# Four passes become one sequence of 64 steps, with the layer's output projection behind them

## What is computed

```
h  = rms_norm(x, g);  xx = token_shift(h) - h
xr, xw, xk, xv, xa, xg = (h + xx * mu[j] for j in range(6))
r, k, v, g = xr @ w_in[0], xk @ w_in[1], xv @ w_in[2], xg @ w_in[3]     # 1024 -> 2048
decay: from w0 + tanh(xw @ w1) @ w2          # low rank 64
a    = sigmoid(a0 + (xa @ a1) @ a2)          # low rank 64
S_t  = S_{t-1} diag(w_t) - (S_{t-1} kk_t)(a_t kk_t)^T + v_t k_t^T;  y_t = S_t r_t   # 32 heads of 64
y    = (head_group_norm(y) + bonus) * silu(g)
x    = x + y @ w_out                          # 2048 -> 1024, the output projection
x    = x + short_conv_mix(rms_norm(x))        # second layer, then further layers
```

## Time and profile before

| | |
|---|---|
| median of three timed runs | 4807.78 us (4807.76 to 4808.15) |
| the profiled execution | 4804.66 us, span of its trace 4802.9 us |
| PE busy | 4343.6 us, 90% of the span |
| DVE busy | 2354.9 us, 49% |
| ACT busy | 1297.8 us, 27% |
| POOL busy | 272.9 us, 6% |
| `rwkv_block` | 0 to about 2593 us of the span |
| DMA queues | 289.75 MB, of it 7.87 MB of instructions (queues q8 and q14) |

### The profile page before, as it was taken

The page is one execution under the profiler, slowest core; times in us unless marked ns, Lnnn a source line. Parts: engine busy times, 40 slices in busy tenths (PEclk is TensorE's granted clock), DMA queues, the critical chain, the costliest instruction groups (busy, mean ns, idle before and its releaser), DMA issues. The chain is left out here.

```text
span 4802.9 us, 134675 instructions
## 1 busy us (share of the span) xinstructions
PE 4343.6 (90%) x58154; PEld 3248.0 (68%) x58154; DVE 2354.9 (49%) x5293; ACT 1297.8 (27%) x3040; POOL 272.9 (6%) x304
## 2 busy tenths in 40 slices
PE   6999989998989998999987999999978988876669
PEld 5888768886478886788853887888755643444444
DVE  4555455553055554555522444344344551588952
ACT  2232223222022332233211333223212321433221
POOL 1000000000000000000000000000000000111100
PEclk9999999998999998999998999999989999567689
DMA  2222222221322221222223332333311110000010
GB/s 70 75 67 66 66 56 67 66 73 58 97 56 75 67 66 48 75 67 66 75 64 97 103 100 83 96 97 96 87 44 29 27 42 9 0 0 1 0 44 35
DMA packets 519184, 289.75 MB, mean 60 GB/s; under 512 B 29008, under 2 KB 508480, under 8 KB 518656
## 3 DMA queue, kind: packets, MB, share of 16 engines
q1 hardware_dynamic: 516352, 277.68, 20.6%
q10 hardware_dynamic: 2304, 4.20, 0.2%
HBM read 271.74 MB, written 8.39 MB: 58 GB/s over the span
## 5 line engine op out<-in xcount | busy, mean ns | idle before, releaser
L348 PE MATMUL a_bank<-a_lerps,a_wt 128*128 128x256 f32 x3072 | 790.6, 393 | 6.2 <-DVE a_lerps L834 2.7
L348 PEld LDWEIGHTS a_bank<-a_lerps,a_wt 128*128 128x128 f32 x3072 | 554.4, 190 | 96.3 <-DVE a_lerps L834 14.0
L1082 PE MATMUL b_bank<-b_hR,b_wR 128*128 128x512 f32 x1024 | 399.9, 391 | 24.7 <-DVE b_wL L1087 24.7
L1082 PE MATMUL b_bank<-b_hR,b_wL 128*128 128x512 f32 x1024 | 399.8, 390 | 0.0
L1082 PE MATMUL b_bank<-b_hL,b_wR 128*128 128x512 f32 x1024 | 399.7, 390 | 0.0
L949 DVE TENSOR_TENSOR a_iv_X<-a_bank,a_iv_X 128x256 f32<-128x256 f32 x256 | 108.7, 425 | 482.8 <-PE a_bank L448 475.6
L348 PE MATMUL a_bank<-a_hT,a_wt 128*128 128x256 f32 x1024 | 264.0, 391 | 0.0
L1087 DVE TENSOR_TENSOR b_wL<-b_w,b_wR 128x1024 fp32r<-128x1024 f32 (+1 forms) x144 | 192.5, 1341 | 117.0 <-ACT b_wR L1177 104.2
L1082 PEld LDWEIGHTS b_bank<-b_hR,b_wR 128*128 128x128 f32 x1024 | 193.2, 189 | 66.3 <-issue 25.9
L708 ACT ACTIVATE a_iv<-a_bank 128x512 f32<-128x512 f32 x192 | 114.6, 597 | 444.0 <-PE a_bank L454 268.1
L628 PE MATMUL a_bank<-a_yT,a_wt 128*128 128x512 f32 x512 | 227.9, 604 | 4.2 <-DVE a_t_sg L1026 4.2
(11 more groups left out here) (449 smaller groups left out, 8110.8 us busy)
## 6 DMA issues: line engine op xcount, KB each, us to landing
a_wt<-in_a_w_in SPq DMA_DIRECT2D x256, 512.0 KB, 4.4
b_w<-in_b_w_in SPq DMA_DIRECT2D x128, 512.0 KB, 4.0
a_wt<-in_a_w_out SPq DMA_DIRECT2D x16, 1024.0 KB, 6.8
b_w<-in_b_w_out SPq DMA_DIRECT2D x16, 1024.0 KB, 5.8
s_wp<-in_w_in SPq DMA_DIRECT2D x12, 512.0 KB, 3.8
a_xtok<-in_x SPq DMA_DIRECT2D x4, 1024.0 KB, 6.8
a_lerps<-in_x SPq DMA_DIRECT2D x2, 2048.0 KB, 9.1
x1t<-a_ends ACTq DMA_DIRECT2D x16, 256.0 KB, 6.1
```

Source lines behind the costliest of these rows:

```text
L348: r = mm(o, wt[:, j, c, :], src[:, c, :], start=(c == 0), stop=(c == ND - 1))
L1082: m = nc.tensor.matmul(o, a, b, start=(first and i == 0), stop=(last and i == 2))
```

## The change

The 64 steps are written out in one sequence (`steps`), with no hardware loops, no register values and no `at_tiles` waits; each step but the last makes the projections of the one after it, across the pass boundaries too. `before` and `first` are left only once, ahead of step 0. The preparation of the next pass is spread over the steps of the current one (`prepared`; `at` is the step's number in its pass): x is loaded at step 3, its squares summed on ACT at 8 (`squares`), the factor made on DVE and POOL and x scaled on DVE at 9, x transposed on PE in four parts at 9 to 12 (`turn_x`), shifted on POOL and mixed on DVE at 10 to 13 (`shift`, `lerped`, now four mixed inputs in a second buffer), and multiplied by the low-rank factors at 14 (`low_in`). The two low-rank products of a step, which had 128 rows each with half of them zeros, have 64 rows each, one on the upper and one on the lower half, and write to banks 0 and 6.

`y` goes to DRAM step by step (`store`, 128 KB). A new `mix_block` behind all steps loads it in 32 chunks of 128x512 through four slots, splits it into R and L parts (one ACT and one DVE instruction each), and makes the output projection for all 1024 tokens: 8 blocks of rows, each in 2 stages of 48 fp32r products, and 8 products for the residual. Beside them it makes the squares and sums for `conv_block`'s norm, whose `x1t` load and norm "1" are gone.

```diff
+        def steps(first, step):
+
+            first(0)
+            for n in range(STEPS):
+                step(n, n % 2, n % NF, n + 1 if n + 1 < STEPS else None, n - 1 if n else None)
+
+        def prepared(n):
+
+            ps, p = n // NF + 1, n % NF
+            return (ps, p) if ps < NPS else (None, None)
...
+                def store(n):
+                    sp.wait_ge(s["tail"], n + 3)
+                    sp.dma_start(yd[n % NF * P:(n % NF + 1) * P, n // NF * PASS:(n // NF + 1) * PASS], ybuf[n % 2][:, :]).then_inc(s[f"yst{n % 2}"], 16)
...
+                    if m >= 3:
+                        store(m - 3)
+                    if m % NF == 3 and m // NF + 1 < NPS:
+                        load_x(m // NF + 1)
...
+                def turn_x(ps, i, bk):
+
+                    pe.wait_ge(s["xsc"], ps + 1)
+                    for c in (2 * i, 2 * i + 1):
                         for b in range(PASS // P):
...
+                            o = c % 2 * PASS + b * P
+                            r = nc.tensor.transpose(bank[bk][:, o:o + P], xtok[:, b, c * P:(c + 1) * P], ident[:, :])
+                    r.then_inc(s["xT"], 1)
...
+                def low_in(ps, lo, hi, bk=0):
+
+                    for c in range(lo, hi):
+                        pe.wait_ge(s["hTe"], ps * ND + c + 1)
+                        mm(bank[bk][:, 0:PASS], lwa1[:, c, :], hT[:, c, 1:PASS + 1], start=(c == 0), stop=False)
+                        r = mm(bank[bk][:, 0:PASS], lwa1m[:, c, :], hT[:, c, 0:PASS], start=False, stop=(c == ND - 1))
+                    if hi == ND:
+                        r.then_inc(s["lwa"], 1)
...
                 def low_rank(m):
                     pe.wait_ge(s["wk"], (m + 1) * 48)
                     pe.wait_ge(s["bdR"], m + 1)
-                    mm(bank[0][:, 0:PASS], lwa2[:, 0, :], hwa[:, :], start=True, stop=True)
-                    mm(bank[0][:, PASS:], lwa2[:, 1, :], hwa[:, :], start=True, stop=True).then_inc(s["pwa"], 1)
+                    pe.wait_ge(s["hwa"], m // NF + 1)
+                    pe.wait_ge(s["hTe"], 2 * turned[0])
+                    if m >= 2:
+                        pe.wait_ge(s["H"], m - 1)
+                    mm(bank[0][:, 0:PASS], lwa2[w_rows, :], hwa[w_rows, :], start=True, stop=True)
+                    mm(bank[6][:, 0:PASS], lwa2[a_rows, :], hwa[a_rows, :], start=True, stop=True).then_inc(s["pwa"], 1)
 
...
+                    if prep and 9 <= at <= 12:
+                        pe.wait_ge(s["bdR"], m + 2)
+                        turn_x(prep, at - 9, 0)
+                        turned[0] += 1
+                    if prep and at == 14:
+                        pe.wait_ge(s["bdR"], m + 2)
+                        low_in(prep, 0, 3)
...
+                def squares(ps):
+                    act.wait_ge(s["xtok"], 16 * ps + 16)
+                    for b in range(PASS // P):
+                        n = ps * (PASS // P) + b
+                        if n:
+                            act.wait_ge(s["x2"], n)
+                        a(junk, xtok[:, b, :], ACT.Square, accum_out=col2["sum"][:, b:b + 1]).then_inc(s["x2"], 1)
+
+                def turned_x(ps, i, bk):
+                    act.wait_ge(s["xT"], ps * (ND // 2) + i + 1)
+                    act.wait_ge(s["hcol"], ps + 1)
+                    for c in (2 * i, 2 * i + 1):
+                        o = c % 2 * PASS
+                        a(hT[:, c, 1:PASS + 1], bank[bk][:, o:o + PASS], ACT.Copy, scale=dcols[:, 0, c:c + 1]).then_inc(s["hTe"], 1)
+
+                def low_out(ps, bk=0):
+                    act.wait_ge(s["lwa"], ps + 1)
+                    if ps:
+                        act.wait_ge(s["pwa"], ps * NF)
+                    a(hwa[a_rows, :], bank[bk][a_rows, 0:PASS], ACT.Copy)
+                    a(hwa[w_rows, :], bank[bk][w_rows, 0:PASS], ACT.Tanh).then_inc(s["hwa"], 1)
...
+                def shift(ps, c):
+                    n = ps * ND + c
+                    pool.wait_ge(s["hTe"], n + 1)
+                    if n >= 2:
+                        pool.wait_ge(s["lerps"], n - 1)
+                    nc.gpsimd.tensor_tensor(xx[c % 2][:, :], hT[:, c, 0:PASS], hT[:, c, 1:PASS + 1], ALU.subtract).then_inc(s["xx"], 1)
+
+                def x_root(ps):
+                    pool.wait_ge(s["xvar"], ps + 1)
+                    nc.gpsimd.tensor_tensor(col2["rstd"][:, :], col2["var"][:, :], k["minus_half"][:, :].to_broadcast([P, PASS // P]), ALU.pow).then_inc(s["xrs"], 1)
...
+                def x_scales(ps):
+                    v.wait_ge(s["x2"], (ps + 1) * (PASS // P))
+                    ts(col2["var"][:, :], col2["sum"][:, :], 1.0 / D, RMS_EPS, ALU.mult, ALU.add).then_inc(s["xvar"], 1)
+                    if ps:
+                        v.wait_ge(s["lwa"], ps)
+                        nc.vector.tensor_copy(hT[:, :, 0], hT[:, :, PASS]).then_inc(s["hcol"], 1)
+                    else:
+                        nc.vector.memset(hT[:, :, 0], 0.0).then_inc(s["hcol"], 1)
+
+                def x_scaled(ps):
+                    v.wait_ge(s["xrs"], ps + 1)
+                    for b in range(PASS // P):
+                        o = ts(xtok[:, b, :], xtok[:, b, :], col2["rstd"][:, b:b + 1], None, ALU.mult)
+                    o.then_inc(s["xsc"], 1)
+
+                def lerped(ps, c):
+                    v.wait_ge(s["xx"], ps * ND + c + 1)
+                    if ps >= 2:
+                        v.wait_ge(s["pv"], (ps - 1) * NF + 1)
+                    for name, j in (("r", 0), ("k", 2), ("v", 3), ("g", 5)):
+                        o = stt(lerp[ps % 2][name][:, c, :], xx[c % 2][:, :], dcols[:, 1 + j, c:c + 1], hT[:, c, 1:PASS + 1], ALU.mult, ALU.add)
+                    o.then_inc(s["lerps"], 1)
...
+                        if n >= 2:
+                            v.wait_ge(s[f"yst{n % 2}"], 16 * (n // 2))
+                        tt(ybuf[n % 2][:, :], t["yn"][:, :], e["gs"][:, :], ALU.mult).then_inc(s["tail"], 1)
...
+                    if prep and at == 9:
+                        x_scaled(prep)
+                    if prep and 10 <= at <= 13:
+                        lerped(prep, 2 * (at - 10))
...
+                    if prep and 10 <= at <= 13:
+                        lerped(prep, 2 * (at - 10) + 1)
...
+def mix_block(nc, d, yd, xT, rs, base):
...
+        chunks = [(h, kq * ND + c) for kq in range(2) for h in range(NHALF) for c in range(ND)]
...
+                for n, (h, c) in enumerate(chunks):
+                    if n == 4:
+                        weights(1)
+                    if n >= 4:
+                        sp.wait_ge(s["yL"], n - 3)
+                    sp.dma_start(slots[n % 4], yd[c * P:(c + 1) * P, tokens(h)]).then_inc(s[f"slot{n % 4}"], 16)
+                for t in range(2, STAGES):
+                    weights(t)
...
+                def squares(c):
+
+                    pe.wait_ge(s["sq"], c + 1)
+                    for h in range(NHALF):
+                        m = nc.tensor.matmul(wide[h][:, :], base["ones"][:, :], sq[:, h, :], start=(c == 0), stop=(c == ND - 1))
+                    m.then_inc(s["sq_used"], 1)
...
+                for t in range(STAGES):
+                    j, kq = divmod(t, 2)
+                    i = t % 2
+                    pe.wait_ge(s["wL"], t + 1)
+                    for h in range(NHALF):
+                        n = j * NHALF + h
+                        o = bank[n % 4]
+                        if n >= 4 and kq == 0:
+                            pe.wait_ge(s["xout"], n - 3)
+                        for c in range(ND):
+                            if j == 0:
+                                pe.wait_ge(s["yL"], (t * NHALF + h) * ND + c + 1)
+                            for q, (a, b) in enumerate(((wR, yR), (wR, yL), (wL, yR))):
+                                r = nc.tensor.matmul(o[:, :], a[i][:, c, :], b[:, kq * ND + c, tokens(h)], start=(kq == 0 and c == 0 and q == 0), stop=False)
+                        if h == NHALF - 1:
+                            r.then_inc(s["stage"], 1)
+                        if kq:
+                            pe.wait_ge(s[f"resid{j % 2}"], 16 * (j // 2) + 16)
+                            for b in range(HALF // P):
+                                r = nc.tensor.matmul(o[:, b * P:(b + 1) * P], resid[j % 2][:, h * (HALF // P) + b, :], base["ident"][:, :], start=False, stop=(b == HALF // P - 1))
+                            r.then_inc(s["pout"], 1)
+                    if j and kq == 0:
+                        squares(j - 1)
+                squares(ND - 1)
...
+    yd = nc.dram_tensor("rwkv_out", (DI, SEQ), F32, kind="Internal").ap()
     with ExitStack() as ctx:
         base = {n: ctx.enter_context(nc.sbuf_tensor("base_" + n, [P, P], F32)) for n in ("ident", "ones")}
-        rwkv_block(nc, d, x1t, base)
+        rwkv_block(nc, d, yd, base)
         xT = ctx.enter_context(nc.sbuf_tensor("xT", [P, ND, SEQ], F32))
-        conv_block(nc, d, x1t, xT, base)
+        with nc.sbuf_tensor("rs", [P, SEQ], F32) as rs:
```

(25 more changed lines are left out.)

480 lines of the change are left out of this document (222 added, 258 removed).

## The result

The changed kernel took 4588.59 us (median of four executions, 4586.48 to 4590.27) beside 4807.97 us for the kernel before on the same chip: a ratio of 0.9543, with a 95% interval from 0.9526 to 0.9559. The profiled execution took 4586.48 us where that of before took 4804.66: 218.2 us less, where the sum had 191.7.

The account below looks back on a forecast made before the run. PE's own list was taken to bound ordinary steps, a bound that breaks at pass boundaries. Terms -292.5 + 25.8 - 12 - 3 + 90.0 = -191.7 took 4807.8 to 4616 us, forecast 4600 to 4632, with two in ten outside 4592 to 4655.

Parts of the forecast that it names:

- I take **-3: Start, up to the first step's end: one reordered preparation saves 3 us, 8 either way, out of 108.1.
- Sixty-three steps at 32.77: From step 0's end to step 63's: steps take 2064.5 of 2357.0 us; the three boundaries' 292.5 all goes.
- so nothing is taken off: Register instructions and always-met waits leave PE's list; counted as no gain, PE being busy 32.7 of 32.77 us.
- preparation in steps: Transposes and low-rank input products on PE add 8.6 us a pass, +25.8; other engines' work costs nothing.
- pair: Two low-rank products on 64-row halves run side by side: 0.78 for 0.97 us, 0.19 less a step, -12.
- end: From the last step's end to the second layer's first product: 264.1 us instead of 174.1, +90.0.
- rival of cheaper instructions: Steps: PE's instructions become cheaper without registers, 0.3 us a step, -19, giving 4597 us; chance 0.08.
- without the change of type it would be 45 more: Output projection: f32 products at 0.86 us in place of three fp32r products would cost 45 us more.
- serial pair: Low-rank products run one behind the other: +0.24 instead of -0.19 a step, +27, 4643 us; chance 0.14.
- slower block: New output projection: chunks at 1.5 us give +10; with slower steps +10 to +35, about 4638; shared chance 0.14.
- late DVE: Steps with a preparation: DVE's cover gone gives up to +20; chance 0.14 shared with the slower new block.
- supply of instructions: PE runs 64 different steps without a loop; at 4 us a step for supply, 4872 us; chance 0.02.

Follow-up runs that it names:

- a4_no_preparation: Changed kernel without load, squares, transposes, low-rank inputs and mixings for the second to fourth pass, which reuse the first pass's; 4564.55 us, ratio 0.9499.
- b2_mixings_together: Changed kernel with both mixings of a step, two times four DVE operations, ahead of X32, where the change has one; 4589.94 us, ratio 0.955.
- c3_pair_between_keys: Changed kernel with the low-rank pair moved behind the first product of the keys, one change of tile size more a step; 4600.64 us, ratio 0.9566.
- a3_extra_waits: Changed kernel with the always-met waits put back on PE, some 25 a step; 4599.05 us, ratio 0.9572.
- b4_twenty_slots: Changed kernel with 20 slots in place of 4 for the chunks of the output projection; 4577.61 us, ratio 0.9526.
- b3_mix_f32: Changed kernel with one f32 product in place of three fp32r products in the output projection, without rounding and rest; 4618.94 us, ratio 0.9609.
- c1_fewer_waits: Changed kernel with nine waits a step taken off PE that an earlier wait implies already; 4584.82 us, ratio 0.9535.
- c2_twenty_slots_fewer_waits: Changed kernel with 20 chunk slots and nine fewer PE waits a step together; 4574.23 us, ratio 0.9509.
- c4_changed_again: The changed kernel itself, run again beside the variants; 4588.42 us, ratio 0.9539.

## Why the prediction was too small

What failed is the sum, in three of its terms: "I take **-3**" for the start, which measured -10.5; "Sixty-three steps at 32.77", which counted the last step as a full one and was 6.2 us too long; and "so nothing is taken off" for registers and waits, where 5.6 came off. Together they are 19.3 of the 26.5 us by which the sum fell short. The first two are sizes, with the mechanism not followed; the third is a wrong reading of a busy share. All terms:

| term | on record | measured in the profiled execution | from |
|---|---|---|---|
| start | -3 | -10.5 | end of the first step, 97.6 for 108.1 |
| boundaries, 63 steps at 32.77 | -292.5 | -292.5 | by definition of the term |
| the last step counted as a full one | 0 | -6.2 | 26.6 for 32.77 |
| preparation in steps | +25.8 | +26.0 | 3 x (4 x 0.44 + 6.91) |
| pair | -12 | -14.3 | 62 x 0.23; the last step has no pair |
| registers and waits | 0 | -5.6 | 62 x 0.09 |
| steps outside the common lengths | 0 | -1.9 | what is left of 2062.5 |
| end | +90.0 | +87.7 | 261.8 less 174.1 |
| behind | 0 | -0.9 | the rest |
| sum | -191.7 | -218.2 | |

*Right: the boundaries.* They held no work that had to come back beyond PE's own, and all 292.5 us went: the steps there now have the lengths of the others.

*Right: the preparation.* 8.67 us a pass beside the 8.6 of the sum, shown by a4_no_preparation and the lengths of steps 9 to 14. DVE's cover, on which the zero for the other engines rested, is real: b2_mixings_together found 1.3 us beside the 1.2 on record, and needed double the mixings to make PE wait at all.

*Right: the pair's mechanism, with the size a little low* (0.19 for 0.23). That it runs side by side is in the records; that it pays for a second change of tile size is shown by c3_pair_between_keys. The 0.13 + 0.11 on record for a change is 0.20 measured. The change of tile size that speaks against the edit was paid, and the edit gained all the same, since 0.43 saved is more than 0.20 paid.

*Wrong: "nothing is taken off" for registers and waits.* That PE was busy for 32.7 of 32.77 us was taken as proof that its list had no gap. It is none: in a3_extra_waits PE counts as busy for 32.45 of 32.45 us though some products start 0.03 to 0.05 us late. The rival of cheaper instructions was right that PE's list had something to give, with three times the size (0.3 for 0.09), and it named the registers, where the waits suffice. The total lies nearer to its 4597 than to 4616, but that is luck: its term is 5.6 of the 26.5 us.

*Wrong in size: the start.* The step that failed is "I take -3". The chain was not followed. Nor are there "eight more mixings": the first pass has 32 on DVE before (24 in line 834, 8 in line 838) and 32 after (line 815). Timeline of the kernel before, the first pass (x was turned first, not yet scaled; then came root, reciprocal and scaling of eight blocks):

```profile
25.20 3.54 PE L311 MATMUL a_bank<-base_ident,a_xtok 128*128 128x128 f32 x16 [8.58 <-DMA a_xtok<-in_x]
...
34.26 1.75 DVE L819 RECIPROCAL a_t_var<-a_t_var 128x256 f32<-128x256 f32 x1 [0.55 <-ACT a_t_var L651]
36.05 3.25 DVE L823 SCALAR_TENSOR_TENSOR a_hT<-a_hT,a_dcols,a_t_var 128x256 f32<-128x256 f32 x8
...
40.54 1.19 PE L323 MATMUL a_bank<-a_hT,a_lwa 128*128 128x256 f32 x2 [7.28 <-POOL a_t_yn L792]
```

And of the changed kernel (two values a partition are rooted, x is scaled, then turned):

```profile
28.67 1.42 DVE L807 TENSOR_SCALAR a_xtok<-a_xtok,a_c_rstd 128x1024 f32<-128x1024 f32 x2 [0.83 <-POOL a_c_rstd L763]
...
30.14 3.68 PE L313 MATMUL a_bank<-base_ident,a_xtok 128*128 128x128 f32 x16 [13.50 <-DVE a_xtok L807]
...
33.61 1.06 PE L320 MATMUL a_bank<-a_hT,a_lwa 128*128 128x256 f32 x2
```

PE's work starts 4.9 us later and its first low-rank product 6.9 us earlier. The wait of 7.28 us between the two has gone; behind it PE ran at the lower clock again, with 0.50 granted from 40.00 to 45.50 us and its records at twice the usual distance. In the changed kernel the granted clock is 1.00 from 30 to 60 us; its records stand at twice the distance once, up to 36.1 us. The low clock at the start of the steps came in both (mean 0.83 from 60 to 70 us now; 0.79 and 0.87 from 70 to 80 us before). This is read from the two traces; no run took it apart, so how much of the 10.5 us is the wait and how much the clock stays open. It also moves from run to run by more than I allowed for: in the profiles of variants with the same start the first step ends at 97.6 to 99.3 us, and the profiled execution of the changed kernel has the lowest.

*Wrong in size: the last step.* "Sixty-three steps at 32.77" counted a step that has no projections left. The last steps of the four passes of before have no projections either; they took 29.39, 34.75, 29.65 and 32.26 us, so the trace said that their length is another one, though none of them gives 26.6. In the changed kernel's variants it is 23.9 to 27.4. What sets it was not taken apart.

*Right: the end*, within 2.3 us of 264.1, and item by item: to the store 5.5 (5.6 to the y on record), to the first DMA 3.7 (3.8), to the first product 6.8 (7.7), chunks 39.5 (37.2 + 0.7), the fourteen stages with the residual and the squares 176.3 (178.9, which has all sixteen residual groups, where two of them lie in the 39.5), the rest 30.0 (30.2). The 1.2 us a chunk was a choice between 1.0 and 1.5, and so in part luck. That four slots set the chunks' pace is shown by b4_twenty_slots. The side remark "without the change of type it would be 45 more" is wrong: 30, since the first two stages are not PE's.

The range missed for one reason: the errors of start, waits and last step were allowed for one by one (8, 19 and nothing) and all went the same way. The rival on the slow side, serial pair, slower block, late DVE, supply of instructions, had 0.30 of the chance; none of it came, unless the short pauses at the end of this text, some 6 us in all, are the last of these.

## What to carry to other kernels

Where one engine's own list sets the time, undoing a boundary was worth its whole length, and what the other engines must do instead is free as far as the trace shows idle time ahead of each of their hand-overs; measure that cover at the place, not over the step. A busy share of 100% does not prove a full list: 26 waits more cost 0.12 us a step with no idle time to be seen, and nine fewer gained nothing, so only a run tells. A stream through few slots runs at its round trip: count slots before engines.

## What the runs showed of the hardware beyond what was expected

- Two f32 products of 64 rows each, with all 128 columns, into two banks start within 0.01 us of each other; 128-row products gain nothing from the same two banks (32.56 us a step, with one bank or two).
- 26 waits a step that were met long before cost PE 0.12 us, nearly all of it at three places.
- Now and then PE pauses inside a group, with no wait that the profile shows. In a3_extra_waits a group of 16 products is cut after 14, and the rest starts 0.64 us late:

```profile
700.62 0.65 PE L400 MATMUL a_bank<-a_dg,a_scr 64*64 64x64 f32 x14
...
701.90 0.32 PE L400 MATMUL a_bank<-a_dg,a_scr 64*64 64x64 f32 x2 [0.64 <-issue]
```

Such pauses make most of what the step's mean (32.42 us without preparation) has above the commonest one, 0.09. No run tells their cause. Two things in the traces point at the supply of instructions. They keep to places in the program: step 7 takes 32.67 to 32.69 us, where 32.33 is common, in both traces of the changed kernel and in those of a4_no_preparation, b2_mixings_together, b3_mix_f32, b4_twenty_slots, c1_fewer_waits and c2_twenty_slots_fewer_waits. And in the changed kernel's trace all 14 pauses of 0.09 us or more that stand out among the steps end 1.7 to 2.8 us after the start of a packet on the instruction queues (q8 and q14), of which one comes every 4.7 us; of all moments about one in five lies so (in c4_changed_again all 16 pauses lie at 1.6 to 2.9 us). It is a correlation, not a shown cause.
